# The mixing part's output product as one float32 product instead of three products of high and low parts

## The reference, cut to what matters

```python
        o = jnp.concatenate([gla_mixer(...), dsa_mixer(...), swa_mixer(...)], axis=-1)
        h = h + o @ w_out[i]
        h = h + hier_moe(rms_norm(h, g_ffn[i]), w_router_group[i], b_router_group[i],
                         w_router_expert[i], b_router_expert[i], ...)
# in hier_moe:
    g_prob = jax.nn.softmax((xt @ w_rg + b_rg).astype(f32), axis=-1)
    e_logits = (xt @ w_re + b_re).astype(f32).reshape(T, N_GROUPS, EXPERTS_PER_GROUP)
```

## Time and profile before

| | us |
|---|---|
| median of 3 runs | 3374.37 |
| the three runs | 3365.84, 3374.37, 3378.43 |
| the profiled execution, its own time | 3367.09 |
| its span, first to last instruction | 3365.4 |
| mix stage in the span, first load issued to last DVE instruction | about 1525 to 1841 |
| PE (TensorE matmul) busy in the span | 2827.1 (84%) |
| DVE, ACT, POOL busy | 1469.5, 1168.0, 652.4 |
| mean granted clock of TensorE | 0.932 of full speed |

### The profile page before, as it was taken

How to read it: one execution, slowest core, us unless ns; L and a number is a source line. 1 busy time by engine, 2 the same in 40 slices (tenths; PEclk the granted TensorE clock), 3 DMA queues, 4 the chain that set the end, 5 groups by cost and what they waited for, 6 DMA issues and landing times. The chain is left out here.

```text
span 3365.4 us, 32920 instructions
## 1 busy us (share of the span) xinstructions
PE 2827.1 (84%) x10296; PEld 1549.2 (46%) x10297; DVE 1469.5 (44%) x2223; ACT 1168.0 (35%) x2093; POOL 652.4 (19%) x862
## 2 busy tenths in 40 slices
PE   7979999889468788874997199999999999997998
PEld 4534333328324344444776044444444444444666
DVE  2267999878966666642222211111111111114565
ACT  2457777649346556642211011110111101112332
POOL 1557787000011111110000400000000000001221
PEclk9989999889779998986998599999999999998999
DMA  5121111111302121214334778646655548613332
GB/s 156 40 50 44 35 41 35 42 40 46 111 31 68 58 93 60 74 54 143 124 112 143 209 264 325 234 175 232 234 194 193 193 163 309 250 51 108 124 128 84
DMA packets 221562, 426.95 MB, mean 127 GB/s; under 512 B 25545, under 2 KB 93833, under 8 KB 221337
## 3 DMA queue, kind: packets, MB, share of 16 engines
q1 hardware_dynamic: 198296, 352.15, 30.8%
q0 software_dynamic: 16256, 48.45, 4.3%
q10 hardware_dynamic: 6912, 25.17, 1.8%
HBM read 326.58 MB, written 99.14 MB: 126 GB/s over the span
## 5 line engine op out<-in xcount | busy, mean ns | idle before, releaser
L535 PE MATMUL p_psP<-home,p_ring 128*128 128x512 f32 (+1 forms) x960 | 431.8, 607 | 28.4 <-ACT p_stage L439 28.4
L2090 PE MATMUL p_psY<-p_wd,p_hT 128*128 x768 | 341.0, 597 | 50.2 <-ACT p_hT L2107 50.2
L2076 PE MATMUL p_psG<-p_wg,p_xT 128*128 x768 | 340.1, 596 | 1.0 <-DVE p_xT L2123 1.0
L2076 PE MATMUL p_psU<-p_wu,p_xT 128*128 x768 | 337.4, 592 | 0.0
L2132 DVE TENSOR_TENSOR p_act_g<-p_act_g,p_psU 128x512 f32<-128x512 f32 x48 | 33.0, 688 | 627.6 <-PE p_psU L2076 627.6
L535 PEld LDWEIGHTS p_psP<-home,p_ring 128*128 128x128 f32 (+1 forms) x960 | 176.7, 187 | 278.2 <-issue 245.3
L2090 PEld LDWEIGHTS p_psY<-p_wd,p_hT 128*128 128x128 f32 x768 | 142.0, 190 | 220.9 <-issue 220.9
L2076 PEld LDWEIGHTS p_psG<-p_wg,p_xT 128*128 128x128 f32 x768 | 146.8, 191 | 186.3 <-issue 186.3
L2076 PEld LDWEIGHTS p_psU<-p_wu,p_xT 128*128 128x128 f32 x768 | 145.9, 190 | 183.7 <-issue 183.7
L2025 POOL TENSOR_TENSOR p_carrier<-p_carrier 128x1 f32<-128x1 f32 x49 | 9.1, 185 | 967.4 <-PE p_psX L2060 963.5
L2136 DVE COPY p_y<-p_psY 128x512 f32<-128x512 f32 x48 | 33.2, 692 | 371.9 <-PE p_psY L2090 371.9
(11 more groups left out here) (345 smaller groups left out, 4866.1 us busy)
## 6 DMA issues: line engine op xcount, KB each, us to landing
p_wg<-in_w_expert_gate_dram SPq DMA_DIRECT2D x32, 2048.0 KB, 9.9
p_wu<-in_w_expert_up_dram SPq DMA_DIRECT2D x32, 2048.0 KB, 16.4
p_wd<-in_w_expert_down_dram SPq DMA_DIRECT2D x32, 2048.0 KB, 12.6
y_dram<-p_y ACTq DMA_DIRECT2D x48, 512.0 KB, 6.4
p_xt<-in_x_dram SPq DMA_DIRECT2D x34, 512.0 KB, 4.1
y_dram<-p_clear SPq DMA_DIRECT2D x32, 512.0 KB, 4.7
proj_f<-p_stage SPq DMA_DIRECT2D x52, 256.0 KB, 2.3
p_ot<-o_dram SPq DMA_DIRECT2D x18, 512.0 KB, 3.8
```

The source lines that it names most:

```text
L535: mm = pe.matmul(psP[0:n, i % 2, :], w, aT[:, k, c * CH:(c + 1) * CH], start=k == 0, stop=k == KD - 1)
L2076: mm = pe.matmul(ps[:, :], xT[:, par, k, :], w_[:, bass.ds(at, 1), k, :].rearrange("p a f -> p (a f)"), start=k == 0, stop=k == KD - 1)
L2090: mm = pe.matmul(psY[:, c, :], hT[:, par, k, :], wd[:, bass.ds(at, 1), k, c * CH:(c + 1) * CH].rearrange("p a f -> p (a f)"), start=k == 0 ...
```

## The change

The four tensors `oT_high`, `oT_low`, `w_high` and `w_low` go, with the instructions that made them. ACT copies a bank of `psT` into `oT` in float32 and raises `oT_done` itself, which DVE did before. The product is one float32 matmul for each n and k, 16 in a tile and 256 in the stage. The loads of `wr`, gain and `br` raise their own semaphore `r_loaded`. PE waits for both semaphores in front of the first product (tile 0) and no more in front of the transpositions; ACT waits for neither; DVE waits for `r_loaded` alone. The order of the loads is the same.

```diff
 def load_mix_weights(sp, weights, w_out, g_ffn, w_rg, b_rg, w_re, b_re):
-    w, wr, br, gain, w_loaded = weights
+    w, wr, br, gain, w_loaded, r_loaded = weights
     for k in range(KD):
         sp.dma_start(w[:, k, :], w_out[0, k * P:(k + 1) * P, :]).then_inc(w_loaded, 16)
-    sp.dma_start(wr[:, :, 0:NG], w_rg[0].rearrange("(k p) n -> p k n", p=P)).then_inc(w_loaded, 16)
+    sp.dma_start(wr[:, :, 0:NG], w_rg[0].rearrange("(k p) n -> p k n", p=P)).then_inc(r_loaded, 16)
...
@@ mix
-        w_high, w_low = sb("w_high", [P, KD, D], F32R), sb("w_low", [P, KD, D], F32R)
-        oT_high, oT_low = sb("oT_high", [P, 2, KD, P], F32R), sb("oT_low", [P, 2, KD, P], F32R)
+        oT = sb("oT", [P, 2, KD, P])
...
             def product(t, par, it):
                 pe.wait_ge(oT_done, t * 2 + 4)
+                if isinstance(t, int) and t == 0:
+                    pe.wait_ge(w_loaded, 16 * KD)
+                    pe.wait_ge(r_loaded, 16 * 5)
                 for n in range(2):
                     if n == 0:
                         pe.wait_ge(h_done, t * 2)
                     c = slice(n * CH, (n + 1) * CH)
-                    product_by_parts(pe, psM[:, n, :], lambda k: (oT_high[:, par, k, :], oT_low[:, par, k, :]),
-                                     lambda k: (w_high[:, k, c], w_low[:, k, c]), KD).then_inc(m_done, 1)
+                    for k in range(KD):
+                        mm = pe.matmul(psM[:, n, :], oT[:, par, k, :], w[:, k, c], start=k == 0, stop=k == KD - 1)
+                    mm.then_inc(m_done, 1)
...
-            pe.wait_ge(w_loaded, 16 * (KD + 5))
-            pe.wait_ge(w_split, KD)
             rotated(pe, (turn, 2), (turn_f, 0), (product, 1), (logits, 0))
...
@@ ACT
-            act.wait_ge(w_loaded, 16 * (KD + 5))
-            for k in range(KD):
-                act.activation(w_high[:, k, :], w[:, k, :], ACT.Copy).then_inc(high_done, 1)
 
             def turn(t, par, it):
                 for b in range(2):
                     act.wait_ge(oT_turned, t * 2 + (b + 1))
-                    act.activation(oT_high[:, par, 4 * b:4 * b + 4, :], psT[:, b, :].rearrange("p (k t) -> p k t", t=P), ACT.Copy).then_inc(oT_highs, 1)
+                    act.activation(oT[:, par, 4 * b:4 * b + 4, :], psT[:, b, :].rearrange("p (k t) -> p k t", t=P), ACT.Copy).then_inc(oT_done, 1)
...
@@ DVE
-            dve.wait_ge(w_loaded, 16 * (KD + 5))
-
-            for k in range(KD):
-                dve.wait_ge(high_done, k + 1)
-                dve.tensor_tensor(w_low[:, k, :], w[:, k, :], w_high[:, k, :].bitcast(F32), ALU.subtract).then_inc(w_split, 1)
-
-            def turn(t, par, it):
-                for b in range(2):
-                    dve.wait_ge(oT_highs, t * 2 + (b + 1))
-                    part = slice(4 * b, 4 * b + 4)
-                    dve.tensor_tensor(oT_low[:, par, part, :], psT[:, b, :].rearrange("p (k t) -> p k t", t=P),
-                                      oT_high[:, par, part, :].bitcast(F32), ALU.subtract).then_inc(oT_done, 1)
+            dve.wait_ge(r_loaded, 16 * 5)
...
-            rotated(dve, (turn, 2), (residual, 1), (norm, 1), (back, 0))
+            rotated(dve, (residual, 1), (norm, 1), (back, 0))
```

More of the change, by code:

```diff
@@ L1552, in mix_weights @@
     gain = ctx.enter_context(nc.sbuf_tensor("p5_gain", [P, D], F32))
-    return w, wr, br, gain, outer.enter_context(nc.semaphore("p5_w_loaded"))
+    return w, wr, br, gain, outer.enter_context(nc.semaphore("p5_w_loaded")), outer.enter_context(nc.semaphore("p5_r_loaded"))
 def load_mix_weights(sp, weights, w_out, g_ffn, w_rg, b_rg, w_re, b_re):
-    w, wr, br, gain, w_loaded = weights
+    w, wr, br, gain, w_loaded, r_loaded = weights
     for k in range(KD):
         sp.dma_start(w[:, k, :], w_out[0, k * P:(k + 1) * P, :]).then_inc(w_loaded, 16)
-    sp.dma_start(wr[:, :, 0:NG], w_rg[0].rearrange("(k p) n -> p k n", p=P)).then_inc(w_loaded, 16)
[L1561 to L1564, removed]
+    sp.dma_start(wr[:, :, 0:NG], w_rg[0].rearrange("(k p) n -> p k n", p=P)).then_inc(r_loaded, 16)
+    sp.dma_start(wr[:, :, NG:NG + NE], w_re[0].rearrange("(k p) n -> p k n", p=P)).then_inc(r_loaded, 16)
+    sp.dma_start(gain[:, :], row_broadcast(g_ffn, D)).then_inc(r_loaded, 16)
+    sp.dma_start(br[:, 0:NG], row_broadcast(b_rg, NG)).then_inc(r_loaded, 16)
+    sp.dma_start(br[:, NG:NG + NE], row_broadcast(b_re, NE)).then_inc(r_loaded, 16)
 def mix(nc, outer, o_dram, x, weights, h_dram, f_dram, ident, router, load_weights):
@@ L1590, in mix @@
         x_loaded = [sem(f"x_loaded{b}") for b in range(2)]
-        high_done = sem("high_done")
-        w_split = sem("w_split")
-        oT_turned, oT_highs, oT_done = sem("oT_turned"), sem("oT_highs"), sem("oT_done")
+        oT_turned, oT_done = sem("oT_turned"), sem("oT_done")
         m_done = sem("m_done")
```

## The result

| | before | changed |
|---|---|---|
| median of 4 runs, us | 3374.86 (3365.84 to 3378.43) | 3408.15 (3404.47 to 3409.36) |
| ratio | | 1.0101 (95% interval 1.008 to 1.0122) |
| the profiled execution, us | 3367.09 | 3408.97 |
| span, us | 3365.4 | 3407.3 |
| mix stage, first `ot` load to the next stage's first load | 316.56 | 355.28 |

The kernel is slower by 33.3 us in the medians (27 to 41 by the interval). The forecast was 3407.1, 32.7 more than before. Times of one kernel differ from run to run by 5 to 15 us, as the ranges in the table show.

What follows compares the result with a forecast made beforehand. PE, busy 84% of the span, was taken to set the pace. 45.3 for the product, minus 14.5 at the start, plus 1.9 cold start gave 32.7 us more: 3374.4 + 32.7 = 3407.1, ratio 1.0097, range 3392 to 3421.

Steps and rivals of the forecast that it cites:

- the product at full clock: Mix stage on PE: 256 float32 products at 0.857 us replace 256 triples at 0.680, costing 45.3 us more.
- start of the first product: Stage start: without the weight split, the first product starts at 1546.66 instead of 1561.18, saving 14.5 us.
- cold start: First product on PE, coming out of a longer idle: 2.9 us lost, 1.9 more than now; bounds 0 and 3.
- low spells in 15 rounds: Low clock in the steady rounds: the 14.4 us lost in 8 long rounds, 1.8 each, stay unchanged.
- end of the stage: Barrier at the stage's end: the next stage begins with its loads, so the whole difference moves to the kernel's end.
- transpositions' cover: Stage start on PE: the first transpositions' 4.2 us lie in the wait for the weights, else return to the path.
- rival C: Rounds of the mix stage: every round gets a low-clock spell, +45.3 us, 3419.7; chance 0.07.
- A: Product on PE: a float32 product takes one pass of a record, 0.429 us; 76.9 us gained, 3297.5; chance 0.02.
- B: Mix stage: full clock is granted throughout, giving back 14.4 of 32.7 us: +18.3, 3392.7; chance 0.07.
- D: Product on PE: float32 passes as long as the split's, 0.227 us, costing 58.1 instead of 45.3, 3419.9; chance 0.03.
- E: Stage start: weights land later or the third `ot` load delays the bias part; at most 5 us less saved, 3412; chance 0.04.
- F: Router: logits differ in last bits, a row changes expert and the block count changes, about 20.6 us a block; chance 0.01.

Runs made afterwards that it cites:

- fourth pass in the split: The kernel before with a fourth matmul, low by low, added to each triple of the split product: 3436.8 us, ratio 1.0187.
- old place of the wait: The changed kernel with PE's wait for the loads put back ahead of the first transpositions: 3417.5 us, 1.0141 of before.
- The filler: Two useless float32 matmuls put on PE before the wait for f: 3384.7 us in the changed kernel, 3353.1 us in the kernel before.
- early product: The changed kernel with its first product waiting for the slices of w alone, the wait for r_loaded behind it: 3402.3 us, ratio 1.0103.

## Why the prediction was right, point by point

The sum, term by term, against the first pair of profiles:

| term | forecast | measured | from |
|---|---|---|---|
| the product at full clock | +45.3 | +45.1 | (19.08 - 16.26) x 16 |
| start of the first product | -14.5 | -13.95 | 22.34 - 36.29 |
| cold start | +1.9 | +1.8 | first product 16.62 against 13.74 warm; 12.04 against 11.0 before |
| low spells in 15 rounds | 0 (-14.4 to +12.6) | +5.3 | 305.95 - 15 x 19.08 = 19.75, before 14.4 |
| end of the stage | 0 | +0.45 | last POOL row to next load, 8.21 against 7.76 |
| the stage | +32.7 | +38.7 | 355.28 - 316.56 |
| outside it | 0 | +3.2 in this pair | 4.3 ahead, -1.1 behind |

**The product.** The step that carried the sum held within 0.2 us. It stood on the count of records in line 535 and the 0.429 us from one to the next in the experts stage. I took 0.857 and not the 0.882 of the finish stage, and 19.08 against the 19.1 forecast says that this was the right row. The fourth pass in the split showed the other price, 0.227 us, apart from the change. The Trainium skill ("FP8 and Floating Point Precision", TensorE Precision Notes) says that true float32 takes four passes. The two records of a product do not show them one by one; its 0.857 us is near the 0.907 of four matmuls of the split, and what the runs add is that it is less (0.214 against 0.227 for a quarter).

**The start.** Right, 0.55 us less than forecast. The bias part took 6.4 us from issue to PE's start (1545.10 to 1551.55) where 5.1 were read before. The third `ot` load issued behind it came to nothing worse. The transpositions' cover was as small as said: without it the first product started 3.4 us later, where 4.2 were named, and took 14.56 us instead of 16.62.

**The low clock.** This term was mis-sized. I left the 14.4 us as they were; they became 19.75. The prediction's rival C had the right picture for the count, since 14 of 15 rounds got a spell (13 in the second profile), but its price was too high. The 1.8 us was a mean: six of the eight long rounds before lost 1.3 to 1.6 us, and two lost 2.7 and 2.8 (in that of 19.09 us the granted clock is still 0.50 over 1732 to 1736). In the changed kernel a spell cost 1.4 us, and even all 15 rounds, as in the experiment with the old place of the wait, came to 6.8 us more than before and not to 12.6. From the fifth round on at the latest the spell falls on the transposition of f and the first records of the product each time.

```profile
1732.00:1736.00 4.00, 4.00 (x14) 0.50 0.77 269
```

The spells need the wait for f, which I had named with the short matmuls as one "thin stretch". The filler took them apart: without the idle 1.65 us there is no spell, with all the short matmuls in place. The other half, the wait without the short matmuls, was not run. Why the rounds lock at 20.48 us, and those of the kernel before and of the four passes do not, these runs do not settle.

**The total.** The stage was 6 us worse than forecast in the first pair of profiles and 4 in the second, and yet the medians met the forecast within 1.1 us. The profiled executions themselves lie 42 and 44 us apart. The part outside the stage, in which the kernels do the same, scatters by more than the miss, so that the medians came so close is luck; what the prediction can claim is the range and the terms of the stage.

**The rivals.** A (one pass) fell with 512 records. B (no spells) fell; its price, +18.3, stood well, for without the 19.75 us of the spells the stage would have been 19.0 us over before (14.9 in the kernel with the filler). D fell with the four passes. E was worth 0.55 us. F: the changed kernel still has 768 records in each product of the experts stage, so the count of blocks did not move.

## What to carry to other kernels

On PE a float32 matmul of 128x512 costs 0.857 us and the three rounded matmuls of the split 0.680, so "one matmul instead of three" loses 0.18 us for each slice where PE sets the pace. Take apart what comes along with such an edit: here the first product starts 14 us earlier, but some 3 of them need only the new place of a wait, and a wait for the weights alone gave the changed kernel 6 more, which the change did not take. And an idle time of PE in every round costs more than its length where the clock falls behind it: here 1.65 us of waiting cost some 3 in a round with a spell, and moving the transposition of f into the next product won 44 us or more, more than the change itself was worth either way.

## What the runs showed of the hardware that I had not expected

- A rounded (fp32r) matmul of 128x512 is 0.227 us from one to the next at full clock, but a quarter of a float32 product is 0.214.
- A wait of 1.65 us in a round of 16.3 to 20.5 us, behind short matmuls, was followed by a fall of the granted clock to 1.2 GHz in 8 of 15 rounds (before) or in 13 and 14 of 15 (changed). Two useless float32 matmuls in its place (1.67 us in the timeline) kept it at 1.00 and made the stage 15 to 16 us shorter (before) and 23 to 24 (changed). A single wait of 3.39 us was followed by such a fall in one kernel and not at once in the other.
- With the float32 product the rounds ran into a steady 20.48 us (within 0.05) in both profiles of the changed kernel, in that with the old start (from the fifth round on) and in that with the early product (from the ninth on). Kernels with rounds of 16.26 or 19.89 us at full clock kept a mixture of long and short ones.
